# A decoder step on one Trainium2 core: the MLP's down product turned round and put on one level of Strassen's scheme

## The reference, cut to what matters

```
x = x + mix @ lw['w_out']
h2 = rms_norm(x, lw['mlp_norm'])
x = x + jnp.square(jax.nn.relu(h2 @ lw['w_mlp_up'])) @ lw['w_mlp_down']
```

## Time and profile before

| | |
|---|---|
| median of 3 runs | 970.32 us (966.54 to 973.47) |
| the profiled execution | 968.15 us |
| its span, first to last instruction | 966.4 us |
| granted TensorE clock, mean | 0.989 |

### The profile page before, as it was taken

How to read it: one execution, slowest core, us unless ns; L and a number is a source line. 1 busy time by engine, 2 the same in 40 slices (tenths; PEclk the granted TensorE clock), 3 DMA queues, 4 the chain that set the end, 5 groups by cost and what they waited for, 6 DMA issues and landing times.

```text
span 966.4 us, 21298 instructions
## 1 busy us (share of the span) xinstructions
PE 924.6 (96%) x8806; PEld 784.0 (81%) x8806; DVE 540.9 (56%) x930; ACT 414.0 (43%) x701; POOL 100.9 (10%) x109
## 2 busy tenths in 40 slices
PE   4999999999999889899999999999999999999998
PEld 3999999999887667675656799978987898789976
DVE  6544576647757843855544754653863386338631
ACT  5235426312242566775355425521751176117610
POOL 0000001114300000000000000003500350026000
PEclk8999999999999999899999999999999999999999
DMA  8222213311202397468995322122322232213212
GB/s 260 67 66 68 66 66 103 104 51 51 81 5 78 128 354 235 143 209 279 349 382 202 137 88 88 44 87 65 110 88 87 55 121 88 87 50 122 93 44 98
DMA packets 63850, 118.33 MB, mean 122 GB/s; under 512 B 5182, under 2 KB 33438, under 8 KB 63754
## 3 DMA queue, kind: packets, MB, share of 16 engines
q1 hardware_dynamic: 60938, 111.68, 34.4%
q0 software_dynamic: 2816, 5.29, 1.7%
HBM read 110.41 MB, written 6.54 MB: 121 GB/s over the span
## 4 chain that ended last, share of the span: by engine, by line
PE 83%; DVE 9%; ACT 3%; DMA 2%; issue 1%; SPq 0%; DVEq 0%; ACTq 0%
PE PS L905 17%; PE PS L906 16%; PE PS L907 16%; PE PS L1066 7%; PE PS L1228 3%; PE PS L1552 3%; PE PS L1298 2%; DVE U L2728 2%; PE PS L1250 2%; PE PS L933 2%; PE PS L1215 2%; PE PS L1334 1%; PE PS L1189 1%; PE PS L1206 1%; PE PS L1436 1%
## 5 line engine op out<-in xcount | busy, mean ns | idle before, releaser
L905 PE MATMUL PS<-WH,U 128*128 128x512 f32 x256 | 101.3, 396 | 0.0
L906 PE MATMUL PS<-WL,U 128*128 128x512 f32 x256 | 99.8, 390 | 0.0
L907 PE MATMUL PS<-WH,U 128*128 128x512 f32 x256 | 99.6, 389 | 0.0
L905 PE MATMUL PS<-WR,HR 128*128 128x384 f32 (+1 forms) x192 | 66.5, 346 | 0.0
L1066 PE MATMUL PS<-AR 64*64 64x64 f32 x1912 | 61.6, 219 | 3.5 <-issue 1.3
L906 PE MATMUL PS<-WR,HR 128*128 128x384 f32 (+1 forms) x192 | 64.6, 336 | 0.0
L2658 DVE TENSOR_TENSOR VQ<-VQ,PS 128x512 f32<-128x512 f32 x40 | 27.4, 687 | 65.9 <-PE PS L907 65.8
L1066 PEld LDWEIGHTS PS<-AR 64*64 64x64 f32 x1912 | 58.6, 135 | 6.8 <-issue 3.9
L1896 ACT ACTIVATE WH<-Wraw 128x2048 fp32r<-128x2048 f32 x18 | 34.3, 1908 | 69.0 <-PE PS L907 68.9
L2675 DVE TENSOR_TENSOR WL<-Wraw,WH 128x2048 fp32r<-128x2048 f32 x18 | 41.3, 2293 | 36.7 <-ACT WH L1896 36.7
L905 PE MATMUL PS<-h2H,WH 128*128 128x288 f32 x208 | 61.4, 295 | 0.0
(11 more groups left out here) (397 smaller groups left out, 2215.0 us busy)
## 6 DMA issues: line engine op xcount, KB each, us to landing
AR<-in_cache_kv SPq DMA_DIRECT2D x120, 384.0 KB, 4.8
Wraw<-in_w_mlp_down SPq DMA_DIRECT2D x16, 1024.0 KB, 5.1
Wraw<-in_w_mlp_up SPq DMA_DIRECT2D x14, 1024.0 KB, 5.4
W<-in_w_in SPq DMA_DIRECT2D x6, 1536.0 KB, 6.5
QK<-in_cache_kv SPq DMA_DIRECT2D x8, 384.0 KB, 6.3
AR<-in_x_prompt SPq DMA_DIRECT2D x4, 512.0 KB, 5.9
Wraw<-in_w_out SPq DMA_DIRECT2D x2, 1024.0 KB, 6.8
VQ<-in_x_prompt SPq DMA_DIRECT2D x4, 512.0 KB, 5.4
```

The source lines that it names most:

```text
L905: mm(out, lH, rH, start=start, stop=False, skip_group_check=skip)
L906: mm(out, lH, rL, start=False, stop=False, skip_group_check=skip)
L907: return mm(out, lL, rH, start=False, stop=stop, skip_group_check=skip)
```

## The change

The down product becomes `quad(i)` as well. There are now 28 quads after the plain up product of round 0: four down quads of round 0, then for each of rounds 1 to 3 four up quads and four down quads (`quad_kind`). In a down quad the w_down block stands as weights (256 output columns, all 1024 hidden columns of the round), and u, in channels by tokens, moves. Its result is the turned output `yT`, summed in SBUF over the rounds.

- **u as an operand of Strassen.** Hidden block pairs of a quad are now the two halves of its contraction. So for each pair the four u quarters need, besides the three that are used plainly (B11, B21, B22), four sums: `sum_u` on DVE makes them by 4 operations of 288, each waiting for the one before. `high` (ACT, 3 x 288) and `high_sums` (ACT, 1 x 1152) make the high parts, `low_ends`, `low_crossed` (DVE, 3 x 288) and `low_sums` (DVE, 1 x 1152) the low ones. They take the place of `square_u` and `quad_low`.
- **Squares in place.** Relu and square are each one operation to a quarter or to the crossed pair. The copy for the sample rows is gone, since they are among the 288 tokens.
- **Operand sums by GpSimd.** The sums of `h2` move from DVE to GpSimd (8 operations of 1152). The weight sums are now made for 28 quads instead of 12. The fourth is written in place and so waits for `form_lo` 2.
- **Partial sums.** In a down quad of rounds 1 to 3 DVE also adds to `yT` (2 operations of 288 and one of 576 more), and the first quarter comes by DVE too. In round 0 they are copied.
- **Residual.** `yT` and the new `relu` lie where `x2` lay. So `x2` is stored to device memory (`x2_home`) before the first relu and loaded back (`x2b`) at the start of the last four quads. PE turns `yT` back at the end (`turn_out`, 40 transposes, 24 of them inside the last quad), DVE adds it to `x2b` (`take_out`) and then the output is stored.
- **Weights.** Each piece is loaded by two DMAs of 512 KB.

The core of the diff:

```diff
+        def u_block(p, which, low):
...
+        def quad_kind(i):
+            r, x = divmod(i + 4, 8)
+            return ("up" if x < 4 else "down"), r, x % 4
...
+            for i in range(NQ):
+                q = i + 4
+                if i:
+                    pool.wait_ge(s_lo, 4 * i)
...
-                tt(S4.rearrange("p (k c) -> p k c", k=4), raw_block(q, 0, 1), s2, SUB).then_inc(s_sum, 1)
...
+                pool.wait_ge(s_lo, 4 * i + 3)
+                tt(raw_block(q, 0, 1), raw_block(q, 0, 1), s2, SUB).then_inc(s_sum, 1)
...
+                first = ((0, plain(0, 0), 0), (1, mixed(3), 3), (2, mixed(2), 1), (3, mixed(1), 2))
+                if kind == "down" and j == 0:
+                    pe.wait_ge(u_dve, 3 * (4 * r + 3))
+                    pe.wait_ge(v_split, 5 + 4 * r + 3)
+                    for n, moving, bank in first:
+                        if n == 2:
+                            forms(1)
+                        product(n, moving, bank, True, range(3))
+                    pe.wait_ge(u_dve, 3 * (4 * r + 3) + 2)
+                    for n, moving, bank in first:
+                        if n == 1:
+                            pe.wait_ge(v_split, 5 + 4 * r + 4)
+                        product(n, moving, bank, False, (3,))
+                    pe.wait_ge(u_dve, 3 * (4 * r + 4))
...
+            for i in range(NQ):
+                kind, r, j = quad_kind(i)
+                was_up = i > 0 and quad_kind(i - 1)[0] == "up"
+                if was_up:
+                    crossed_quarters(i - 1)
+                copy_p1(i)
+                if was_up and kind == "down":
+                    high_sums(pair_no(i - 1))
+                form_hi(i, 3)
+                if was_up and kind == "up":
+                    high_sums(pair_no(i - 1))
+                if i < NQ - 1:
+                    form_hi(i + 1, 0)
+                    form_hi(i + 1, 1)
+                if i < 4:
+                    act.wait_ge(t_sum, 5)
+                    f(t_block(TF, i), t_block(Tf, 4 + i), ACT.Copy).then_inc(t_hi, 1)
+                if kind == "up":
+                    last_quarter(i)
+                if kind == "up" or r == 0:
+                    first_quarter(i)
+                if i < NQ - 1:
+                    form_hi(i + 1, 2)
...
+            def sum_u(n):
+
+                r0a, r0b, r1a, r1b = (relu[:, r, c:c + 288] for r in range(2) for c in (0, 288))
+                t1, t2, t3, t4 = (Vf[:, 8 * (n % 4) + 4 + x, :] for x in range(4))
+                dve.wait_ge(u_act, squared(n))
+                link(tt(t1, r0b, r0a, SUB))
+                link(tt(t2, r1b, t1, SUB))
+                link(tt(t3, r1b, r0b, SUB))
+                tt(t4, r1a, t2, SUB).then_inc(u_dve, 1)
```

More of the change, by code:

```diff
@@ L551, in pair_free, with relu_at, squared, copied @@
         def pair_free(i, p):
-            r, j = i // 4 + 1, i % 4
-            return pair_used(i - 1, p) if j else mlp_used(8 * r - 2 + p // 2)
+            return pair_used(i - 1, p) if i else (u_ps, 6 + p // 2 * 2)
+        def relu_at(f):
+            return f + f // 2 + 1
+        def squared(n):
+            return 3 * n + 3 if n < 4 else 9 + n
+        def copied(i):
+            return sum(2 - (quad_kind(x)[0] == "down" and quad_kind(x)[1] > 0) for x in range(i))
         def form(ring, n):
@@ L1470, in quad, with product @@
             def quad(i):
[L1472 to L1475 removed]
+                kind, r, j = quad_kind(i)
+                def product(n, moving, bank, start, ks=range(4)):
                     wH, wL = form(WH, n), form(WL, n)
[L1478 to L1481 removed]
+                    out = bank288(i, bank)
+                    for k in ks:
+                        last = mm3(out, (wH[:, k, :], wL[:, k, :]), moving(k), start and k == 0, k == 3, skip=not start or len(ks) < 4)
+                    if 3 in ks:
+                        last.then_inc(g_ps, 1)
@@ L1562, in _, with y_at, turn_out @@
-            down(0)
-            for r in range(1, NR):
-                for j in range(4):
-                    quad(4 * (r - 1) + j)
-                down(r)
+                product(6, plain(1, 1), 2, False)
+            def y_at(t, k):
+                if t == 4 or k < 6:
+                    return (t % 2 * 2 if t < 4 else 0) * 512 + k * 128
+                return (4 + t) * 512 + (k - 6) * 128
+            def turn_out(t, ks):
+                t0, nr = TILES[t]
+                if t in (2, 3) and 0 in ks:
+                    pe.wait_ge(resid_ev, 10 + t - 1)
+                elif t == 4:
+                    pe.wait_ge(resid_ev, 13)
+                for k in ks:
+                    last = turn(PS[0:nr, y_at(t, k):y_at(t, k) + 128], yT[:, k, t0:t0 + nr], ident)
+                last.then_inc(turned, 1)
@@ L1569, in _ @@
+            for i in range(NQ):
+                quad(i)
+            pe.wait_ge(c_sum, 4 * NQ)
+            turn_out(4, range(8))
+            for t in range(4):
+                turn_out(t, range(6, 8))
         @block.scalar
@@ L1946, in form_hi, with high, high_sums @@
                 ins.then_inc(s_hi, 1)
+            def high(n, which):
+                src = (relu[:, 0, 0:288], relu[:, 1, 0:288], relu[:, 1, 288:T])[which]
+                f(u_block(n % 4, which, 0), src, ACT.Copy).then_inc(u_hi, 1)
+            def high_sums(n):
+                act.wait_ge(u_dve, 3 * n + 1)
+                f(u_sums(VF, n % 4, 0), u_sums(Vf, n % 4, 1), ACT.Copy).then_inc(u_hi, 1)
             def copy_p1(i):
@@ new lines, in _ @@
+                r = relu[:, n % 2, :]
+                f(halves(r), pair(n % 4), ACT.Relu).then_inc(u_act, 1)
+                act.wait_ge(u_act, relu_at(n))
+                if n % 2 == 0:
+                    link(f(r, r, ACT.Square))
+                    if p == 2:
+                        act.wait_ge(t_sum, 1)
+                    high(p, B11)
+                else:
+                    f(r, r, ACT.Square).then_inc(u_act, 1)
+                    act.wait_ge(u_act, squared(p))
+                    high(p, B22)
+                    high(p, B21)
+                    if n < 4:
+                        split_hi(p + 2)
+                    if n == 5:
+                        form_hi(0, 0)
+                        form_hi(0, 1)
+                    high_sums(p)
@@ new lines, in partial_sums @@
+                if kind == "up":
+                    dve.wait_ge(u_hi, 4 * pair_no(i))
+                elif r:
+                    link(tt(dst, dst, U3, ADD))
+                dve.wait_ge(g_ps, 7 * i + 4)
+                tt(dst, bank288(i, 2), U3 if kind == "up" or not r else dst, ADD).then_inc(c_sum, 1)
+                if kind == "down" and r:
+                    both = yT[:, 2 * j:2 * j + 2, :].rearrange("p d t -> p (d t)")[:, 288:864].rearrange("p (r t) -> p r t", r=2)
+                    link(tt(both, both, U2.unsqueeze(1).to_broadcast([128, 2, 288]), ADD))
@@ L2845, in _channels @@
+            take_out(2, 2, range(6))
+            take_out(3, 3, range(6))
+            crossed_sums(NQ - 1)
+            take_out(4, 4, range(8))
+            for t in range(4):
+                take_out(5 + t, t, range(6, 8))
 def _channels(a, n):
```

566 lines of the change are left out of this document (247 added, 319 removed).

## The result

The changed kernel takes 1049.2 us (median of 4 runs, 1047.9 to 1053.2) against 971.05 us for the kernel before on the same chip (4 runs): a ratio of 1.082, 95% interval 1.077 to 1.087. The forecast was 1050 us. The profiled execution of the changed kernel has a span of 1051.5 us and a time of 1053.24, so about 1.75 us lie around the span, as before.

What follows compares the result with a forecast made beforehand. The prediction took the up quads to be bound by a loop over ACT and DVE, the down quads mostly by PE. From 673.6 us, rounds of 120.4, a partial last round and an end of 26.2 gave 1050 us, range 1003 to 1070.

Steps and rivals of the forecast that it cites:

- The loop of the up quads: Nine up quads behind an up quad: the loop over ACT and DVE takes 17.4 us, taken as 17.5, against 11.53.
- The first up quad: First up quad of a round (three): both quarters stand behind form steps that wait for GpSimd, 12.5 us.
- The first down quad: First down quad of rounds 1 to 3: PE idle 4.8 and 3.2 us, 22.0 us with the lower clock.
- The other down quads: Down quads after the first of a round: PE's pace, 11.15 us each, bounds 11.1 and 11.9.
- Round 0: Before the first up quad of round 1: first down quad 4.9 us late, loop 11.7; the 7.4 us saved are lost.
- The end: Last quad, turning back, additions and output store: 26.2 us from the last quad's start.
- The clock: PE idle some 5 us in up quads, then granted clock 0.50 for about 3.4 us, mostly hidden in PE's wait.
- GpSimd cheap: Rival: GpSimd takes little from DVE, up quads 13.8 instead of 17.5, 1012 us; chance 0.28 together with a shorter loop.
- The low clock that stays: Rival: PE stays at 1.2 GHz through the up quads, which take 22 us, 1090 us in all; chance 0.07.
- Hidden: Rival: ACT and DVE run far enough ahead that each quad keeps PE's pace, 961 us; chance 0.05.
- The shorter loop: Rival: small operations overlap, up quad 15 us, first down quad 18, 1016 us; chance 0.28 together with GpSimd cheap.
- The count that spoke against it: Up quads: two-input DVE operations 8.6 us plus GpSimd's 5.2, 13.8 together, over PE's 11.1; set against the hidden rival.

Runs made afterwards that it cites:

- the run with tiny sums: The changed kernel with GpSimd's four weight sums a quad cut from 512 to 16 elements: 1002.0 us.
- the filler matmuls: The changed kernel with 40 matmuls of unused result on PE in every up quad behind another, before its wait for U3: 1050.2 us.
- the reordering: DVE's and ACT's orders changed, sums' high part ahead of P1's copy, early store, on the changed kernel with GpSimd's weight sums cut to 16 elements: 998.6 us.
- the kernel with the high part of the sums first: The changed kernel with ACT's high part of the operand sums ahead of the copy of P1 in the first down quads: 1039.5 us.

## Why the prediction was right

The forecast of 1050 us met 1049.2, and the mechanism did too: the length of each kind of quad came within 1 us of the walk. That the total fits to 1 us is partly luck, as the terms below miss both ways, and the forecast left out 1.8 us that its own sum had (1051.8). Step 2 of the first up quads of rounds 1, 2 and 3 was due at 673.6, 794.0 and 914.4 and came at 677.3, 797.2 and 916.7; that of the last quad was due at 1023.8 and came at 1025.1. So 3.7 us at the start (of which 5.0 is the unchanged part ahead, which the walk can't know, and -1.3 round 0) were partly made up by rounds 0.5 to 1.0 us shorter than said.

- *The loop of the up quads.* Zero is step 2 at 707.37 in the third up quad. The walk said: low part of the last form done at 6.45, the seven operations and turns at 13.2, U3 at 14.1, next step 2 at 17.4. The trace has 6.99 (713.67 + 0.69), 12.97, 13.83 and 17.27 (724.64). So the last form came 0.5 us late and the stretch behind it was 0.9 us shorter than walked; the two nearly cancel. Of the two estimates under it, 0.45 for 288 elements with two SBUF inputs alone was met. The three turns were put at 3.6 us; the three long sums are 2.9 us longer than alone (1.43 against 0.45), and the run with tiny sums gives 3.4 a quad. The three such quads of a round were put at 52.5 us and took 51.2 and 51.1, since the first of them took 16.7.
- *The first up quad*, 12.5 us by the walk: step 2 to step 2 took 13.4 in round 1 and 13.0 in round 2. It was too low by 0.5 to 0.9.
- *The first down quad*, 22.0: 21.5. The two waits of PE are where they were put, 2.45 and 2.94 us where the walk had 4.8 and 3.2. The first was oversized since PE came out of the last up quad later than at 0.2; the first product still began at 5.1 (746.94 less 741.86), where the walk had it at 5.0, so the sum hardly moved.
- *The other down quads*, 33.45 for three: 33.9. PE's saving is real there: 11.05 us where a down segment took 12.98. In the first of the three GpSimd's chain is a little longer than PE (11.7).
- *Round 0.* By the walk DVE's sums of the third pair began at 613.4, the first down quad was 4.9 us late, and its successors ran at 11.7. With the 5.0 us by which the unchanged part came later, that is what happened: DVE began at 618.2, its first sum took 2.58 us beside one of GpSimd's of 1152 elements, PE stood 4.1 us, and the loop ran at 11.7. One wait was missing from the walk. PE was done with round 0 at 675.8 and stood until 678.7 for the low part of the last sum of `h2` (L2750 on DVE). It cost little, since step 2 had come at 677.3: the first up quad of round 1 took 13.4 us against 13.0 in the other rounds.
- *The end*, 26.2: 26.4 from step 2 at 1025.1 to 1051.5.
- *A round*, 120.4: 119.9 and 119.4.
- *The clock*: idle of 3.1 us (the walk had some 5; the nine waits for U3 have a mean of 4.0) was followed by 0.50, as was said, but it stayed there for 6.8 us in seven of the nine quads and 10.2 in two, not the 3.4 of the estimate from the earlier trace rows. That this costs at most 0.5 us a quad is shown by the filler matmuls.

The rivals: GpSimd cheap (1012) falls with the three sums at 1.43 and with the 47 us that its sums cost. The low clock that stays (1090) falls, since it was back at 1.00 in each quad. Hidden (961) falls: DVE ended at 13.0, not 8.0. The shorter loop (1016) falls with 17.2 us in an up quad, where it had 15, and 21.3 in the first down quad, where it had 18. The count that spoke against it, 13.8 us of DVE's and GpSimd's exclusive work in a quad of 11.1, was no more than an argument, and the runs bear it out only in part: no version without omissions came under 15.3 us in an up quad behind another, and the wait that the reordering brought in hides how near to 13.8 one could come.

In the Trainium skill, "SBUF — State Buffer", section "Who interferes with whom", a DVE instruction with two SBUF inputs and a GpSimd instruction that reads SBUF exclude each other. The trace agrees (0.45 against 1.43). U2 and U3, with one input in PSUM, took 0.45 and 0.46, but in that quad GpSimd was done by then, so these two rows don't show what one SBUF input does. The crossed sums do: they too have one input in PSUM, and at 710.15 they took 0.76 us with GpSimd's fourth sum of 512 elements running beside them (the row below), and 0.75 in the kernel in which that sum has 16 elements:

```profile
709.81 1.29 POOL L903 TENSOR_TENSOR Wraw<-Wraw,rc 128x512 f32<-128x512 f32 x1 [8.29 <-DVE WL L2758]
```

## What to carry to other kernels

Fewer matmul columns are worth their time only while PE is what the others wait for; here the saving of 2 us in a down quad was real and 9 of 12 up quads paid 5.7 us each for its operands. Before putting work on DVE beside GpSimd, or the other way round, count what DVE does with two SBUF inputs in the same stretch and add the two: here they took turns by whole instructions, and the busy shares of 63% and 20% don't show it. To find what a wait is worth, follow the loop around and move its parts together; taking away the one place where PE waits gave nothing, and a reordering of my own made a new loop out of a wait that had cost nothing. And compare the parts, not only the totals: with tiny sums the reordering gave 19 us in one place and lost 22 in another.

## What the runs showed of the hardware that I had not expected

- A turn lasted until the other engine's instruction was done, at both of its sizes: a DVE sum of 288 elements, 0.45 us alone, took 1.43 beside a GpSimd sum of 512 and 2.58 beside one of 1152 (four of these took 10.84 us).
- The granted clock fell to 0.50 after an idle time of 3.1 us and was 1.00 again only 6.8 us later (720.3 to 727.1), with PE busy from 721.3 on, twice as long as around 343 us in the kernel before. In the kernel with the high part of the sums first, an idle time of 3.2 us in the third up quad of round 2 (831.8 to 835.0) was followed by no fall at all. What decides it was not tried.
